# A streaming encoder step on one core: second-norm stage re-ordered, last taps and low parts on GpSimd, y rows ordered by expert block

## The chip, the core and the metric

The kernel is written for one core of one Trainium2 chip. A core has TensorE (matrix products into PSUM), VectorE, ScalarE, GpSimd and SyncE, which issues most DMAs. The engines run their own instruction streams and wait for each other on semaphores. In the views they are PE (PEld for its weight loads), DVE, ACT, POOL and SP; a queue name with a q behind it is that engine's sequencer or DMA queue. The metric is the device time of one launch in microseconds.

## What is computed

One layer with pre-norms, 1088 tokens (1024 of a prompt, 64 of a sample) of width 1024, all in fp32:

```
z = rms_norm(x, norm1_g) @ w_in                       # 512 pooling, 512 value, 512 gate columns
y_pool, _ = pool_mix(z[:, :512], ...)                 # window means, per-group linear, scale
v = a * sigmoid(gate); h = depthwise_conv(v, width 31) + b
y_conv = swish(layer_norm(h))
x = x + concat(y_pool, y_conv) @ w_out + b_out
hm = rms_norm(x, norm2_g)
# top 1 of 4 groups, then top 2 of its 8 experts; p_grp * normalised top_p are the gates
y = sum over the two chosen experts e of gate_e * ((silu(hm @ w_eg[e]) * (hm @ w_eu[e])) @ w_ed[e])
out = rms_norm(x + y, norm_f_g)
```

The last rows of the pooling input and of the convolution input are outputs too.

## The kernel before

Tokens are tiled by 128 rows: `NT` = 9 tiles, the last of 64. A product of two fp32 matrices is made of three: each operand is split into a high part (ScalarE copies it to the PE's format) and a low part (value less high part, by VectorE or GpSimd), and TensorE adds high x high, high x low and low x high. So every weight and every activation costs ScalarE a copy and another engine a subtraction.

Each engine's program is written out by hand; nothing is scheduled by a tool. The stages:

- **Input projection.** `turn_x(t)` transposes the nine normalised tiles; `in_proj(j, n)` multiplies column chunk j (12 of 128 columns, `KINDS`) with token block n (512, 512, 64). `in_proj(0, 0)` stands inside the loop of the transposes, all others after it. Chunks 0 and 1 use different PSUM banks.
- **Convolution.** Four groups of 128 channels, 31 taps. VectorE runs the taps of the parts `PART` by `taps`, one instruction a tap. For the ranges in `HELPED`, ScalarE makes the products of a tap (`products`) and GpSimd adds them (`additions`), with three product buffers `taps_pr` and the semaphores `prod_done` and `help_done`. Before, part C (group 1, its last 206 columns) is VectorE's.
- **Second-norm stage** (about 225 to 419 us). For each tile `out_conv(t)` and `out_pool(t)` make the output projection, 24 products each, from the parts in `part_h[t % 2]` and `part_l[t % 2]`. `residual(t)` (VectorE, L1256) adds x; ScalarE takes the sum of squares (L679) and the root (L682), written in the loop over t; `hm_row(t)` (L1263, L1268) scales the row; `turn_hm(t)` (TensorE, L943) transposes it; `hm_turned(t)` (ScalarE, L656) copies it out of PSUM; `logits(t)` (L954) are the router's products. `route(t)` and `count(t)` on VectorE find the two experts; `ranks(t)` (L964, L965) counts the rows ahead; `place(t)` (L1317 to L1335) turns ranks to slots; `slot_table` gathers all of it. `mix_high(t)` (ScalarE, L644, L650), `mix_conv_low(t)` and `mix_pool_low(t)` (VectorE, L1221, L1227) make the parts of tile t. The LayerNorm of token blocks 1 and 2 stands in the same stage: `ln_mean` (L817), `ln_center`, `ln_square`, `ln_variance` (L825), `ln_deviation`, `ln_normal`, `ln_swish`. `ln_mean(1)` waits for all taps. In the loop, TensorE makes `logits(t - 2)` and `ranks(t - 3)` after the output projection of tile t.
- **Experts.** 32 blocks of 128 rows, one for each expert; further blocks only if an expert has more than 128 rows (none here). `pair_loop` runs 15 passes of two blocks, then reads the number of pairs, then runs nine passes whose body is skipped, then a last pair is finished outside. TensorE works on one block after the other; its down projection is L1035 to L1037. GpSimd gathers rows for a block from `hm_scratch` (L1639) and scatters results (L1644) to `y2_dram`, where row 2 x token + k is the token's k-th expert.
- **Tail.** SyncE waits for `sc_all`, which GpSimd raises when the last scatter has landed, and loads both y rows of a tile with one DMA (`load_y2`, eight buffers). `combine(t)` (L1496) adds gate times row twice, ScalarE takes squares and root (L767, L770), `final(t)` (L1503, L1505) scales, SyncE stores.

## Time and profile before

| | us |
|---|---|
| median of 3 runs | 1084.33 (1083.77 to 1084.92) |
| the profiled execution | 1084.51 |
| its span, first to last instruction | 1082.8 |
| PE busy | 933.9 (86%) |
| DVE busy | 877.2 (81%) |
| ACT busy | 622.4 (57%) |
| POOL busy | 262.3 (24%) |
| mean granted TensorE clock | 0.927 of full speed |

A timeline row gives start and busy time of one instruction or of several alike (x count); what stands in brackets is the idle time of that engine ahead of it and the engine, tile and line whose work ended the wait. "issue" is time in which the profile shows nothing waited for. Groups by line give the total and the mean of one instruction. PEclk is the part of TensorE's full clock (2.4 GHz) that was granted; at half of it a product on 512 columns follows the last after 0.43 us, at full after 0.23.

### The profile page before, as it was taken

The page shows a single profiled execution, that of the slowest core. Times are in us where ns is not written, and L with a number is a line of the kernel's source. Part 1 is how long each engine was busy: PE and PEld are TensorE (multiplying, and loading weights), DVE is VectorE, ACT ScalarE, POOL GpSimd, SP SyncE. Part 2 cuts the span into 40 slices and gives each one's busy share as a digit, 9 for nine tenths or more (in the row PEclk, how much of TensorE's full clock was granted, in tenths as well). Part 3 has the DMA queues.
Part 4 walks back from the last instruction along what each step waited for, and adds up shares of the span by engine and source line. Part 5 has one row for each costly group of instructions (what it writes and reads, how often), then busy time and mean ns, then how long its engine had stood idle before and what let it go on. Part 6 is the DMA issues. An engine that isn't in the chain of part 4 may idle for free.

```text
span 1082.8 us, 13490 instructions
## 1 busy us (share of the span) xinstructions
PE 933.9 (86%) x4446; PEld 766.9 (71%) x4446; DVE 877.2 (81%) x974; ACT 622.4 (57%) x592; POOL 262.3 (24%) x284
## 2 busy tenths in 40 slices
PE   4999999791699983979999999999999999999710
PEld 3788888570468872768888888888888888888500
DVE  6279998979647875989898989898988989898248
ACT  7245353530232222747878787878787878887223
POOL 2158688350001101032212121212121111111000
PEclk8999999996889985889999999999999999999865
DMA  8211111131116242789999999999999999999466
GB/s 262 84 53 35 37 35 59 26 112 39 74 43 233 107 175 85 239 295 391 375 390 375 395 382 398 389 386 387 382 384 373 386 380 385 375 385 349 158 271 232
DMA packets 66299, 268.63 MB, mean 248 GB/s; under 512 B 15215, under 2 KB 28015, under 8 KB 40601
## 3 DMA queue, kind: packets, MB, share of 16 engines
q1 hardware_dynamic: 56761, 250.36, 61.9%
q0 software_dynamic: 9504, 17.85, 4.3%
q8 instruction: 18, 0.29, 0.1%
q14 instruction: 16, 0.13, 0.0%
HBM read 254.09 MB, written 30.86 MB: 263 GB/s over the span
## 4 chain that ended last, share of the span: by engine, by line
PE 81%; DVE 8%; issue 4%; ACT 3%; DMA 2%; SPq 0%; DVEq 0%; POOLq 0%; POOL 0%; ACTq 0%
PE ps L1021 11%; PE ps L1023 11%; PE ps L1022 11%; PE ps L899 8%; PE ps L1035 6%; PE ps L1036 6%; PE ps L1037 6%; PE ps L779 5%; PE ps L780 5%; PE ps L781 5%; PE ps L1010 3%; DVE arena L1496 2%; DVE ps L1155 2%; PE ps L1042 1%; PE ps L954 1%
## 5 line engine op out<-in xcount | busy, mean ns | idle before, releaser
L704 ACT ACTIVATE big<-arena 128x2048 fp32r<-128x2048 f32 x192 | 363.1, 1914 | 70.6 <-PE ps L1037 36.9
L1431 DVE TENSOR_TENSOR low<-arena,big 128x2048 fp32r<-128x2048 f32 x126 | 285.2, 2286 | 39.9 <-ACT big L704 37.2
L1021 PE MATMUL ps<-big,ring 128*128 128x512 f32 x512 | 205.5, 401 | 2.4 <-DVE ring L1436 2.4
L1023 PE MATMUL ps<-big,ring 128*128 128x512 f32 x512 | 201.2, 393 | 0.0
L1431 DVE TENSOR_TENSOR big<-arena,big 128x2048 fp32r<-128x2048 f32 x66 | 151.0, 2289 | 18.1 <-ACT big L704 14.7
L1155 DVE SCALAR_TENSOR_TENSOR ps<-arena,cols,ps 128x512 f32<-128x512 f32 (+1 forms) x174 | 137.2, 788 | 6.0
L1021 PEld LDWEIGHTS ps<-big,ring 128*128 128x128 f32 x512 | 97.0, 189 | 22.6 <-DVE ring L1436 2.8
L1023 PEld LDWEIGHTS ps<-big,ring 128*128 128x128 f32 x512 | 96.8, 189 | 22.5
L899 PE MATMUL ps<-big,ring 128*128 128x512 f32 (+1 forms) x432 | 104.7, 402 | 8.4 <-ACT arena L591 3.9
L1035 PE MATMUL ps<-big,hT 128*128 128x512 f32 x256 | 103.0, 402 | 8.9 <-DVE hT L1446 8.9
L779 PE MATMUL ps<-big,ring 128*128 128x512 f32 (+1 forms) x288 | 104.0, 361 | 0.4 <-DVE big L1119 0.4
L780 PE MATMUL ps<-big,ring 128*128 128x512 f32 (+1 forms) x288 | 102.7, 357 | 0.0
L781 PE MATMUL ps<-big,ring 128*128 128x512 f32 (+1 forms) x288 | 102.0, 355 | 0.0
L899 PEld LDWEIGHTS ps<-big,ring 128*128 128x128 f32 (+1 forms) x432 | 80.2, 188 | 30.7 <-ACT arena L591 4.7
L1037 PE MATMUL ps<-big,hT 128*128 128x512 f32 x256 | 101.9, 398 | 0.0
L1022 PE MATMUL ps<-low,ring 128*128 128x512 f32 x256 | 100.7, 394 | 0.0
L1022 PE MATMUL ps<-big,ring 128*128 128x512 f32 x256 | 100.6, 393 | 0.0
L1036 PE MATMUL ps<-low,hT 128*128 128x512 f32 x248 | 98.6, 397 | 0.0
L1661 POOL COPY cur<-s_idx 128x1 uint32 x32 | 16.7, 523 | 325.3 <-ACT arena L722 325.3
L1609 POOL TENSOR_TENSOR arena<-arena 128x606 f32<-128x606 f32 (+1 forms) x60 | 70.8, 1180 | 7.8 <-POOL arena L1609 0.4
L679 ACT ACTIVATE arena<-arena 128x1024 f32<-128x1024 f32 (+1 forms) x9 | 9.5, 1059 | 105.7 <-DVE arena L1256 84.0
L1035 PEld LDWEIGHTS ps<-big,hT 128*128 128x128 f32 x256 | 49.0, 191 | 20.9 <-DVE hT L1446 7.5
(228 smaller groups left out, 1409.2 us busy)
## 6 DMA issues: line engine op xcount, KB each, us to landing
arena<-in_w_eg SPq DMA_DIRECT2D x64, 1024.0 KB, 7.6
arena<-in_w_eu SPq DMA_DIRECT2D x64, 1024.0 KB, 7.0
arena<-in_w_ed SPq DMA_DIRECT2D x64, 1024.0 KB, 7.2
arena<-in_x_prompt SPq DMA_DIRECT2D x16, 512.0 KB, 5.4
y_in<-y_scratch SPq DMA_DIRECT2D x8, 1024.0 KB, 12.7
arena<-in_w_in SPq DMA_DIRECT2D x12, 512.0 KB, 3.6
arena<-in_w_out SPq DMA_DIRECT2D x8, 512.0 KB, 4.0
x_scratch<-arena SPq DMA_DIRECT2D x8, 512.0 KB, 2.6
```

What stands on the lines that cost most here:

```text
L704: act.activation(we_h[n % RING], raw[n % RING], ACT.Copy).then_inc(high_done, 1)
L779: pe.matmul(out, sh, mh, start=(i == 0), stop=False)
L780: pe.matmul(out, sh, ml, start=False, stop=False)
L899: ins = pe.matmul(out_ps[t % 2][0:r, c0:c0 + BANK], sh[t % 2][:, k, 0:r], mv[:, k, c0:c0 + BANK], start=(first and k == rows[0] and i == 0 ...
L1021: pe.matmul(out, part_h[b][:, k, :], wh[:, q, :], start=(k == 0), stop=False)
L1022: pe.matmul(out, part_h[b][:, k, :], wl[:, q, :], start=False, stop=False)
L1023: ins = pe.matmul(out, part_l[b][:, k, :], wh[:, q, :], start=False, stop=(k == KD - 1))
L1035: pe.matmul(out, hT_h[:, k, :], wh[:, q, c0:c0 + BANK], start=(k == 0), stop=False)
L1036: pe.matmul(out, hT_h[:, k, :], wl[:, q, c0:c0 + BANK], start=False, stop=False)
L1037: ins = pe.matmul(out, hT_l[:, k, :], wh[:, q, c0:c0 + BANK], start=False, stop=(k == KF - 1))
L1155: dve.scalar_tensor_tensor(to, v_ext[:, c, a + j:b + j], cols[:, c, j:j + 1], run, ALU.mult, ALU.add).then_inc(conv_step, 1)
L1431: dve.tensor_tensor(we_l[n % RING], raw[n % RING], we_h[n % RING].bitcast(F32), ALU.subtract).then_inc(low_done, 1)
```

## The change

1. `HELPED` has a third range, the former part C: its products are ScalarE's (31, in two pieces around the first row deviation) and its sums GpSimd's (13 and 17 additions, ahead of the additions of `b_out` to tiles 1 and 2). They use three product buffers of their own.
2. `in_proj(1, 0)` stands ahead of the transposes of the last tile.
3. The order of the second-norm stage is written out on TensorE, ScalarE and VectorE. The taps of group 3 are cut otherwise (8, 5, 18 instead of 10, 21), the low parts of tile 2 stand before the last 18. The LayerNorm means come after `out_pool(2)`. `logits(t - 1)` stands behind `out_pool(t)` from tile 5 on. The low parts of tiles 4 to 8 are made by GpSimd (`mix_low`).
4. In `place`, the two rows of a token are exchanged (`swap`, `rowv`) where the first expert's block has the higher number, so that k = 0 is always the lower block; seven instructions exchange the gates accordingly.
5. `pair_loop` enters the further passes only if there is one.
6. The tail loads the k = 0 rows of all tiles once all scatters but the last have landed, and the k = 1 rows after the last; `combine` is cut in two, nine additions for k = 0 first. 18 buffers instead of 8.

```diff
@@ -157,10 +159,13 @@
-FB = 8
...
-y_in = [place(f"y_in{s}", AT_BIG + s * HP, 2 * D)[:, :] for s in range(FB)]
+y_at = [[AT_BIG + (2 + t // 2) * HP + (t % 2) * D for t in range(NT - 1)] + [AT_ARENA + LOW_AT[1] * HP],
+        [AT_BIG + (0, 1, 6, 7)[t // 2] * HP + (t % 2) * D for t in range(NT - 1)] + [AT_ARENA + LOW_AT[1] * HP + D]]
+y_in = [[place(f"y_in{k}_{t}", y_at[k][t], D)[:, :] for t in range(NT)] for k in range(2)]
@@ -296,8 +303,8 @@
-PART = {"A": (0, BANK), "B": (BANK, HW_), "C": (CUT, HW_)}
-HELPED = [(0, BANK, HW_), (1, BANK, CUT)]
+PART = {"A": (0, BANK), "B": (BANK, HW_)}
+HELPED = [(0, BANK, HW_), (1, BANK, CUT), (1, CUT, HW_)]
@@ -336,10 +343,13 @@
-    with eng.Fori(PAIRS - 1, MAX_PAIRS - 1) as i:
-        with eng.If(rest > i):
-            body(i, True)
+    with eng.If(rest > PAIRS - 1):
+        with eng.Fori(PAIRS - 1, MAX_PAIRS - 1) as i:
+            with eng.If(rest > i):
+                body(i, True)
+            eng.nop()
...
+    eng.nop()
@@ -480,18 +490,18 @@
-    def load_y2(t):
-        r = ROWS[t]
-        sp.dma_start(y_in[t % FB][0:r, :], y2_dram[2 * t * P:2 * (t * P + r), :]
-                     .rearrange("(p k) n -> p (k n)", k=2)).then_inc(f_in[t % FB], 16)
...
+    def load_y2(k, t):
+        src = y2_dram[2 * t * P:2 * (t * P + ROWS[t]), :].rearrange("(p k) n -> p k n", k=2)[:, k, :]
+        sp.dma_start(y_in[k][t][0:ROWS[t], :], src).then_inc(f_in[k][t], 16)
...
+    sp.wait_ge(scat, 32 * rest + 32)
+    for t in range(NT):
+        load_y2(0, t)
...
-    for t in range(FB):
-        load_y2(t)
     for t in range(NT):
-        if t + FB < NT:
-            sp.wait_ge(f_acc, 2 * t + 2)
-            load_y2(t + FB)
+        load_y2(1, t)
+    for t in range(NT):
@@ -564,7 +574,7 @@
-                act.wait_ge(help_done, TAPS)
+                act.wait_ge(help_done, h * TAPS)
         for j in range(made[h], made[h] + n):
@@ -573,7 +583,7 @@
-                act.activation(taps_pr[j % 3][:, 0:b - a], v_ext[:, c, a + j:b + j], ACT.Copy,
+                act.activation(taps_pr[3 * (h == 2) + j % 3][:, 0:b - a], v_ext[:, c, a + j:b + j], ACT.Copy,
@@ -669,31 +679,43 @@
     for t in (0, 1):
...
-    for t in range(NT):
+    def row_deviation(t):
...
-        if t in (0, 2):
-            act.wait_ge(var_done, t + 1)
-        act.activation(junk[0:r, :], xt[t % 2][0:r, :], ACT.Square,
-                       accum_out=stat[0:r, 3, t:t + 1]).then_inc(sum2_done, 1)
+        if t == 4:
+            act.wait_ge(var_done, 3)
+        to = junk_h if t < 4 else junk
+        act.activation(to[0:r, :], xt[t % 2][0:r, :], ACT.Square, accum_out=stat[0:r, 3, t:t + 1]).then_inc(sum2_done, 1)
...
-        if t == 1:
-            mix_high(t + 2)
-            ln_square(1)
-            ln_square(2)
-        if t == 2:
-            ln_deviation(1)
-            ln_deviation(2)
-        if t >= 1:
-            hm_turned(t - 1)
-        if t == 2:
-            ln_swish(1)
-            ln_swish(2)
-        if t != 1 and t + 2 < NT:
...
+    products(2, 14)
+    row_deviation(0)
+    mix_high(2)
+    products(2, TAPS - 14)
+    row_deviation(1)
+    mix_high(3)
+    ln_square(1)
+    ln_square(2)
+    hm_turned(0)
+    row_deviation(2)
+    ln_deviation(1)
+    ln_deviation(2)
+    ln_swish(1)
+    ln_swish(2)
+    mix_high(4)
+    row_deviation(3)
+    hm_turned(1)
+    mix_high(5)
+    hm_turned(2)
+    for t in range(4, NT):
+        row_deviation(t)
+        hm_turned(t - 1)
+        if t + 2 < NT:
@@ -837,10 +859,14 @@
+        if t == NT - 2:
+            pe.wait_ge(wl_done, 2)
+            pe.wait_ge(cols_done, 1)
+            in_proj(1, 0)
     for n in (1, 2):
...
-    pe.wait_ge(cols_done, 1)
...
     def taken(j):
@@ -854,7 +880,7 @@
-        for n in range(3):
+        for n in range(1 if j == 1 else 0, 3):
@@ -978,29 +1004,56 @@
-    for t in range(NT + 3):
-        if 2 <= t < NT:
-            out_conv(t)
-            out_pool(t)
-        if t == 2:
-            pe.wait_ge(yp_dve, 3)
-            pe.wait_ge(conv_done, 3)
-            pe.wait_ge(help_done, 2 * TAPS)
-            ln_mean(1)
-            ln_mean(2)
-        if 3 <= t < NT + 2:
-            logits(t - 2)
-        if 1 <= t <= NT:
-            turn_hm(t - 1)
-        if t == 2:
-            pe.wait_ge(cen_done, 3)
-            ln_variance(1)
-            ln_variance(2)
-            logits(0)
-        if t == NT + 1:
-            slot_table("own", 0, 2 * NT - 6)
-        if t >= 3:
-            ranks(t - 3)
+    out_conv(2)
+    out_pool(2)
+    pe.wait_ge(yp_dve, 3)
+    pe.wait_ge(conv_done, 2)
+    pe.wait_ge(help_done, 3 * TAPS)
+    ln_mean(1)
+    ln_mean(2)
+    turn_hm(0)
+    out_conv(3)
+    pe.wait_ge(cen_done, 3)
+    ln_variance(1)
+    ln_variance(2)
+    out_pool(3)
+    logits(0)
+    turn_hm(1)
+    out_conv(4)
+    logits(1)
+    turn_hm(2)
+    out_pool(4)
+    logits(2)
+    turn_hm(3)
+    out_conv(5)
+    logits(3)
+    ranks(0)
+    turn_hm(4)
+    out_pool(5)
+    logits(4)
+    ranks(1)
...
+    out_pool(8)
+    logits(7)
+    ranks(6)
+    turn_hm(8)
+    logits(8)
+    slot_table("own", 0, 2 * NT - 6)
+    ranks(7)
+    ranks(8)
...
     def turn_rows(blk):
@@ -1247,7 +1300,7 @@
-    taps(10, ("B", 3))
+    taps(8, ("B", 3))
     def residual(t):
@@ -1329,44 +1382,77 @@
+        step(dve.tensor_tensor(swap[:, t:t + 1], s_b[:, a:a + 1], s_b[:, a + 1:b], ALU.is_gt))
+        dve.tensor_tensor(rowv[:, a:a + 1], tokv[:, a:a + 1], swap[:, t:t + 1], ALU.add)
+        step(dve.tensor_tensor(rowv[:, a + 1:b], tokv[:, a + 1:b], swap[:, t:t + 1], ALU.subtract))
...
         for s in (a, b - 1):
-            ins = dve.tensor_scalar(hots[s], iota[:, :], lane[:, s:s + 1], tokv[:, s:s + 1], ALU.is_equal,
+            ins = dve.tensor_scalar(hots[s], iota[:, :], lane[:, s:s + 1], rowv[:, s:s + 1], ALU.is_equal,
...
-    for t in range(NT + 3):
-        if t == 2:
-            ln_center(1)
-            ln_center(2)
-        if t < NT:
-            residual(t)
-            hm_row(t)
-        if t == 0:
-            pooled_sample()
-            taps(TAPS - 10, ("B", 3))
-            dve.wait_ge(conv_step, steps[0])
-            dve.engine_nop().then_inc(conv_done, 1)
-            taps(10, ("C", 1))
-        if t == 1:
-            taps(TAPS - 10, ("C", 1))
-            dve.wait_ge(conv_step, steps[0])
-            dve.engine_nop().then_inc(conv_done, 1)
-        if t == 2:
-            ln_normal(1)
-            ln_normal(2)
-        if t + 2 < NT:
-            mix_conv_low(t + 2)
-            mix_pool_low(t + 2)
-        if 2 <= t < NT + 2:
-            route(t - 2)
-            count(t - 2)
-        if t >= 3:
-            place(t - 3)
...
+    residual(0)
+    hm_row(0)
+    pooled_sample()
+    taps(5, ("B", 3))
+    mix_conv_low(2)
+    mix_pool_low(2)
+    taps(TAPS - 13, ("B", 3))
+    dve.wait_ge(conv_step, steps[0])
+    dve.engine_nop().then_inc(conv_done, 1)
+    residual(1)
+    hm_row(1)
+    mix_conv_low(3)
+    mix_pool_low(3)
+    ln_center(1)
+    ln_center(2)
+    residual(2)
+    hm_row(2)
+    ln_normal(1)
+    ln_normal(2)
+    residual(3)
+    route(0)
+    count(0)
+    hm_row(3)
+    route(1)
+    count(1)
+    residual(4)
+    hm_row(4)
+    route(2)
+    count(2)
+    route(3)
+    count(3)
...
+    residual(8)
+    place(5)
+    hm_row(8)
+    route(7)
+    count(7)
+    place(6)
+    route(8)
+    count(8)
+    place(7)
+    place(8)
     def slots(a, b):
@@ -1421,6 +1507,14 @@
+        step(dve.tensor_tensor(gtmp[:, 0, :], gates[:, 1, :], swap[:, :], ALU.mult))
+        step(dve.tensor_tensor(gtmp[:, 1, :], gates[:, 0, :], swap[:, :], ALU.mult))
+        step(dve.tensor_scalar(swap[:, :], swap[:, :], -1.0, 1.0, ALU.mult, ALU.add))
+        dve.tensor_tensor(gates[:, 0, :], gates[:, 0, :], swap[:, :], ALU.mult)
+        step(dve.tensor_tensor(gates[:, 1, :], gates[:, 1, :], swap[:, :], ALU.mult))
+        dve.tensor_tensor(gates[:, 0, :], gates[:, 0, :], gtmp[:, 0, :], ALU.add)
+        step(dve.tensor_tensor(gates[:, 1, :], gates[:, 1, :], gtmp[:, 1, :], ALU.add))
@@ -1488,14 +1582,15 @@
-    def combine(t):
-        r, s = ROWS[t], t % FB
-        dve.wait_ge(f_x[t], 16)
-        dve.wait_ge(f_in[s], 16 * (t // FB + 1))
-        for k in range(2):
-            dve.scalar_tensor_tensor(x_in[t][0:r, :], y_in[s][0:r, k * D:(k + 1) * D], gates[0:r, k, t:t + 1],
-                                     x_in[t][0:r, :], ALU.mult, ALU.add).then_inc(f_acc, 1)
-            dve.wait_ge(f_acc, 2 * t + k + 1)
+    def combine(k, t):
+        r = ROWS[t]
+        if k == 0:
+            dve.wait_ge(f_x[t], 16)
+        else:
+            dve.wait_ge(f_acc, t + 1)
+        dve.wait_ge(f_in[k][t], 16)
+        dve.scalar_tensor_tensor(x_in[t][0:r, :], y_in[k][t][0:r, :], gates[0:r, k, t:t + 1],
+                                 x_in[t][0:r, :], ALU.mult, ALU.add).then_inc(f_acc, 1)
     def final(t):
@@ -1621,10 +1718,26 @@
     for q in POOL_WO:
...
+    def mix_low(t):
+        r, tok = ROWS[t], t * P
+        pool.wait_ge(mixc_high, t + 1)
+        pool.tensor_tensor(part_l[t % 2][:, NG:KD, 0:r], hc[:, :, hc_at(tok):hc_at(tok) + r],
+                           part_h[t % 2][:, NG:KD, 0:r].bitcast(F32), ALU.subtract).then_inc(mixc_low, 1)
+        pool.wait_ge(mh_done, t + 1)
+        pool.tensor_tensor(part_l[t % 2][:, 0:NG, 0:r], u_ext[:, :, tok:tok + r],
+                           part_h[t % 2][:, 0:NG, 0:r].bitcast(F32), ALU.subtract).then_inc(ml_done, 1)
...
     for t in range(NT):
...
+        if t == 1:
+            additions(2, 13)
+        if t == 2:
+            additions(2, TAPS - 14)
+        if t >= 4:
+            mix_low(t)
```

Line numbers of the changed kernel differ: L925 is the output projection (L899 before), L980 the logits (L954), L969 the transposes of the norm row (L943), L990 and L991 the ranks (L964, L965), L691 and L693 square and root (L679, L682), L666 the copy `hm_turned` (L656), L654 and L660 the high parts, L495 the y loads.

TensorE's stream at tile 6, before: the output projection, the logits of tile 4, the transposes of tile 5, the ranks of tile 3.

```order
L899 MATMUL ps<-big,ring 128x512 [waits x2_done,mixc_low]
L899 MATMUL ps<-big,ring 128x512 x23
L899 MATMUL ps<-big,ring 128x512 [waits ml_done]
L899 MATMUL ps<-big,ring 128x512 x23
L954 MATMUL ps<-w_rt,arena 128x36 [waits lg_read,hmT_done]
L954 MATMUL ps<-w_rt,arena 128x36 x7
L943 MATMUL ps<-ident,arena 128x128 [waits hmT_done,hm_done]
L943 MATMUL ps<-ident,arena 128x128 x7
L964 MATMUL ps<-MS,tri 128x32 [waits placed,counted]
L965 MATMUL ps<-pref,ones 128x32
```

The same engine around tile 6 in the changed kernel, from `out_pool(5)` on: the logits that follow are those of the tile before (4, behind tile 5's products).

```order
L925 MATMUL ps<-big,ring 128x512 [waits ml_done]
L925 MATMUL ps<-big,ring 128x512 x23
L980 MATMUL ps<-w_rt,arena 128x36 [waits lg_read,hmT_done]
L980 MATMUL ps<-w_rt,arena 128x36 x7
L990 MATMUL ps<-MS,tri 128x32 [waits placed,counted]
L991 MATMUL ps<-pref,ones 128x32
L925 MATMUL ps<-big,ring 128x512 [waits x2_done,mixc_low]
L925 MATMUL ps<-big,ring 128x512 x23
L990 MATMUL ps<-MS,tri 128x32 [waits placed,counted]
L991 MATMUL ps<-pref,ones 128x32
L969 MATMUL ps<-ident,arena 128x128 [waits hmT_done,hm_done]
L969 MATMUL ps<-ident,arena 128x128 x7
```

Logits and ranks moved ahead by one tile, and the logits that follow a tile's products read a copy made later than before. That copy on ScalarE, changed kernel, tile 5: square and root of tile 5, then the copy of tile 4's transposed row, then the high parts of tile 7.

```order
L691 ACTIVATE arena,stat<-arena 128x1024 [waits sum2_done,x2_done]
L693 ACTIVATE stat<-stat,eps 128x1 [waits sum2_done]
L666 ACTIVATE arena<-ps 128x1024 [waits lg_done,hmtr_done]
L654 ACTIVATE ring<-arena 128x512 [waits out_done,mix_done]
L660 ACTIVATE ring<-arena 128x512
```

ScalarE's order inside a tile did not change there: the copy stands behind the square, which waits for the residual (`x2_done`).

SyncE's stream in the tail, before: both y rows of a tile in one load, all after the last scatter.

```order
L481 DMA bo_bc<-in_norm_f_g 128x1024
L485 DMA y_in_60<-y_scratch 128x2048 [waits scattered]
L485 DMA y_in_61<-y_scratch 128x2048
L485 DMA y_in_62<-y_scratch 128x2048
...
L485 DMA y_in_60<-y_scratch 64x2048 [waits f_acc]
L497 DMA out<-arena 128x1024 [waits f_y] x8
L497 DMA out<-x_last 64x1024 [waits f_y]
```

And in the changed kernel: nine loads wait for the scatter's count, nine for the last scatter.

```order
L491 DMA bo_bc<-in_norm_f_g 128x1024
L498 ISA
L495 DMA y_in_0_61<-y_scratch 128x1024 [waits scat]
L495 DMA y_in_1_62<-y_scratch 128x1024
...
L495 DMA y_in_8_69<-y_scratch 64x1024
L495 DMA y_in_0_70<-y_scratch 128x1024 [waits scattered]
L495 DMA y_in_1_71<-y_scratch 128x1024
...
L495 DMA y_in_8_78<-y_scratch 64x1024
L507 DMA out<-arena 128x1024 [waits f_y] x8
L507 DMA out<-x_last 64x1024 [waits f_y]
```

The first half of the loads moved ahead of the last scatter; each load is half as large.

## Rows read from the trace of the kernel before

**Rows 1.** Windows: length, busy PE, PEld, DVE, ACT, POOL (count), PEclk, DMA, GB/s.
```profile
36.00:206.00 170.00, 168.37 (x868) 140.83 (x866) 134.03 (x173) 67.78 (x100) 116.39 (x101) 0.99 0.12 36
232.00:297.00 65.00, 32.73 (x128) 24.32 (x126) 53.11 (x75) 8.83 (x14) 7.97 (x4) 0.79 0.13 51
...
325.00:419.00 94.00, 84.91 (x463) 71.60 (x461) 74.61 (x291) 28.57 (x41) 11.69 (x6) 0.90 0.40 149
484.00:1003.00 519.00, 519.00 (x2436) 428.97 (x2434) 464.70 (x261) 413.29 (x304) 89.88 (x118) 1.00 0.99 382
...
1031.00:1083.00 52.00, 0.46 (x2) 0.02 (x1) 35.50 (x36) 15.20 (x29) 1.16 (x2) 0.53 0.68 262
```

**Rows 2.** Timeline of PE at the head.
```profile
32.05 1.91 PE L792 MATMUL ps<-ident,arena 128*128 128x128 f32 x16
35.55 0.68 PE L792 MATMUL ps<-ident,arena 64*128 64x64 f32 x8 [1.59 <-DVE big L1119]
36.58 0.51 PE L779 MATMUL ps<-big,ring 128*128 128x512 f32 x1 [0.36 <-DVE big L1119]
...
38.19 0.63 PE L781 MATMUL ps<-big,ring 128*128 128x512 f32 x1
```

**Rows 3.** Timeline of PE around the second norm.
```profile
269.47 12.88 PE L899 MATMUL ps<-big,ring 128*128 128x512 f32 x48 [3.15 <-DVE ring L1221]
286.78 6.12 PE L817 MATMUL ps<-arena,mean_w 128*128 128x512 f32 x16 [4.44 <-issue]
...
325.94 11.25 PE L899 MATMUL ps<-big,ring 128*128 128x512 f32 x48
337.03 1.87 PE L954 MATMUL ps<-w_rt,arena 128*128 128x36 f32 x16
```

**Rows 4.** Groups by line and form, taps: count | busy us, mean ns | idle before.
```profile
L1609 POOL TENSOR_TENSOR arena<-arena 128x606 f32<-128x606 f32 x30 | 42.5, 1416 | 3.6
...
L1609 POOL TENSOR_TENSOR arena<-arena 128x400 f32<-128x400 f32 x30 | 28.3, 944 | 4.2 <-POOL arena L1609 0.4
...
L1155 DVE SCALAR_TENSOR_TENSOR arena<-arena,cols 128x206 f32<-128x206 f32 x30 | 15.0, 500 | 1.0
```

**Rows 5.** Timeline of DVE and ACT after the last tile's output projection.
```profile
393.41 1.22 DVE L1256 TENSOR_TENSOR arena<-ps,arena 64x1024 f32<-64x1024 f32 x1 [2.21 <-PE ps L899]
...
394.66 1.06 ACT L679 ACTIVATE arena<-arena 64x1024 f32<-64x1024 f32 x1 [10.36 <-DVE arena L1256]
...
396.04 1.00 ACT L656 ACTIVATE arena<-ps 128x1024 f32<-128x1024 f32 x1
```

**Rows 6.** Timeline of DVE, first read of the slot table.
```profile
418.69 0.19 DVE L1373 TENSOR_SCALAR idx_f<-ps 128x32 f32<-128x32 f32 x1 [0.70 <-PE ps L977]
```

**Rows 7.** Timeline of PE, first down projection.
```profile
470.69 0.80 PE L1035 MATMUL ps<-big,hT 128*128 128x512 f32 x1 [7.45 <-DVE hT L1446]
```

**Rows 8.** Timeline of all engines, loop exit to the first y tile.
```profile
1002.25 1.92 ACT L704 ACTIVATE big<-arena 128x2048 fp32r<-128x2048 f32 x1 [1.82 <-issue]
...
1017.71 0.98 POOL L1644 DMA_INDIRECT y_scratch<-arena,cur  x1 [0.83 <-POOL cur L1661]
...
1021.62 1.11 PE L1042 MATMUL ps<-ident,arena 128*128 128x128 f32 x4 [6.22 <-issue]
...
1034.08 0.97 POOL L1644 DMA_INDIRECT y_scratch<-arena,cur  x1 [0.81 <-POOL cur L1661]
...
1037.37 8.38 SPq L485 DMA_DIRECT2D y_in<-y_scratch  x9
...
1042.66 5.25 DVE L1496 SCALAR_TENSOR_TENSOR arena<-y_in,gates,arena 128x1024 f32<-128x1024 f32 x4 [18.57 <-DMA y_in<-y_scratch]
```

**Rows 9.** Timeline of DVE, a tile of the tail.
```profile
1049.56 2.60 DVE L1496 SCALAR_TENSOR_TENSOR arena<-y_in,gates,arena 128x1024 f32<-128x1024 f32 x2
...
1052.39 1.28 DVE L1505 SCALAR_TENSOR_TENSOR arena<-arena,stat,bo_bc 128x1024 f32<-128x1024 f32 x1
```

**Rows 10.** Timeline of DVE, a cast of a placing step.
```profile
349.94 2.29 DVE L1325 CAST sl<-sl_i 128x2 f32<-128x2 int32 x1
```

More of the change, by code:

```diff
@@ L1150, in taps @@
                         j = at_tap.get((part, c), 0)
[L1151 removed]
+                        run = acc_ps[:, 0:b - a]
                         if j:
@@ new lines, in _ @@
+            ln_normal(2)
[11 more added lines that the diff above has]
+            count(3)
+            residual(5)
+            place(0)
+            hm_row(5)
+            place(1)
+            route(4)
+            count(4)
+            residual(6)
+            place(2)
+            hm_row(6)
```

47 lines of the change are left out of this document (37 added, 10 removed).

## The prediction

> **What bounds the kernel now.** I read the busy times of stretches first [rows 1]. In 36 to 206 us (input projection) TensorE is busy 168.4 of 170 us: whatever starts it earlier moves everything behind it. In 484 to 1003 us (30 of 32 expert blocks) it is busy 519 of 519 us at a granted clock of 1.00, and no line of that loop's body changes. What is left is slack: 232 to 297 us holds 32.7 us of TensorE work in 65, with VectorE at 53.1; 325 to 419 us runs at 84.9 of 94; 1031 to 1083 us is a tail in which only VectorE (35.5) and ScalarE (15.2) work. So the change is priced in four places, as shifts of the chain. Times are those of the trace of before. The profiled execution took 1084.51 us (span 1082.8), the median is 1084.33: the sum is made against 1084.5, and the 0.2 between them is nothing here.
>
> **Head: one product moved ahead of the last transposes.** TensorE ends the transposes of tiles 6 and 7 at 33.96, idles 1.59, turns tile 8, idles 0.36, and its next eight or so products run at a start-to-start distance of 0.43 us, not 0.23 (durations 0.63 for 0.39) [rows 2]. With in_proj(1, 0) put there, 24 products (5.5 us) fill the wait for tile 8. Its inputs are ready (low part of chunk 1 at 27.7 us). Removed: 1.95 us of idle and 8 x 0.2 = 1.6 us of half clock, together 3.6. The bounds are 1.9 (clock falls anyway) and 3.8. The sigmoid, the weight parts and VectorE's gating of chunk 0 start 1.8 us later and still come before chunk 2 needs them (ready 54.2, needed 56.5). All of 36 to 206 us follows TensorE, so I take **-3.6**.
>
> **Second-norm stage, first half.** TensorE starts the LayerNorm means at 286.78 after 4.4 us of idle [rows 3], released by VectorE's taps of part C. These are 30 taps of 0.50 us and a first one [rows 4], 16.4 us with their spacing; they leave VectorE. The second tile's residual, its wait and its norm row (1.22 + 1.54 + 2.1, the first two as in [rows 5]) move behind the means: 4.9 more. Against it, ScalarE now makes 14 products before the first row deviation, in step with GpSimd: its 10th addition must be over. An addition on 206 elements I take from the two widths [rows 4]: busy 1.416 us at 606 and 0.944 at 400 is 2.3 ns an element, so 0.50, and 0.62 with the gap seen between them; GpSimd starts at 232.6, so ScalarE is free at 239.3, 0.8 late for x2. Means at 286.8 - 16.4 - 4.9 + 0.8 = 266.3. GpSimd's 30 additions end at 235 + 30 x 0.62 = 253.6, 12 us before they are asked for. Their cover is that; they cost nothing up to 1.03 us each.
>
> From 266.3 I go forward with durations of before: means 6.1, one transpose 1 to 2, out_conv(3) 5.7 (end 280), variance 3.9, out_pool(3) (289.4), logits 1.7. Beside it VectorE: residual(1), norm row(1), low parts(3), centring to 275.6, reciprocal and scaling 284.2 to 290.8. ScalarE: swish to 294.1, high part of tile 4. GpSimd now makes the low part of tile 4, 1.25 us (half of its 2.4 for 1024 elements), so out_conv(4) starts at 296.1 after 4 us of idle. Before it started at 325.94 [rows 3]: **-29.9** to this point.
>
> **Second half: routing one tile behind.** Before, the steady tile is 14.07 us: 48 products 11.1, logits 1.7, transposes 0.9, ranks 0.4 [rows 3], and logits(t-2) after out_pool(t) find their input long ready. Now logits(t-1) follow out_pool(t), while ScalarE's order is still row_deviation(t), hm_turned(t-1). So for t = 5, 6, 7, 8 TensorE waits for residual(t), square, root and copy, of which all but the copy belong to a tile it has only just finished. This chain is in the trace once, at tile 8: the residual starts at 393.41 as the products end, the square at 394.66, the copy runs 396.04 to 397.04 [rows 5]: 3.7 to 3.9 us. In 5, 6 and 7 (the fourth stands in the tail) it is 11.7 us. After idles of 2.5 to 4.4 us the next products run at half clock for a while: 48 of them took 12.88 after 3.15 us idle and 11.25 without [rows 3], +1.6. I charge that after each of three stalls and at out_conv(4): 6.4, with 0.6 for slower logits. From out_conv(4) to the end of out_pool(8) TensorE then has 5 x 11.1 products, 6 each of logits, transposes and ranks (18.4, where before had 4 sets, 12.1), 11.7 of stalls and 7.0 of clock: 92 against 67.3 before, **+24.6**.
>
> From there VectorE is the chain: residual, place(5), norm row, route(7), place(6), route(8), place(7), place(8). Before it takes 25.3 us to the table's reading at 418.69 [rows 6], with one route and one place more; each place now has three instructions more, two dependent steps, 0.5 us. The sum is 22.3: **-3.0**. The stage as a whole: -29.9 + 24.6 - 3.0 = **-8.3** (the gather and the first experts follow the table as before).
>
> The seven new instructions on the gates stand ahead of the low part that ends in the hidden low part for which TensorE waited 7.45 us [rows 7]. Five steps of 0.21 and two of 0.07 by their neighbours (0.17 busy): **+1.2**.
>
> **Loop exit and tail.** Between its last loop product (1015.4) and 1021.62 TensorE's sequencer runs nine skipped passes, 6.22 us; ScalarE passes the same nine in 1.82 [rows 8]. The fixed part (leaving, loading the count) is at most those 1.82; one guard replaces nine passes, so it gives 8/9 of 6.22 - 1.82 to 6.22: 3.9 to 5.5, I take 4.7. The Trainium skill (Advanced Engine Details and Errata, Control Flow Timing) gives 108 ns for a compare-and-branch and 51 ns for a branch, from which I estimate 1.4 us for nine passes and a gain of 1.3: the row shows four times that on TensorE, and by the page the time would be 3.4 us higher.
>
> Then: last scatter issued by 1035.05 before, now 1030.1; landed 2.3 us later, as before (1037.37), so 1032.4, and the second halves of y are asked for. The first halves wait only for the scatter of the block before, issued by 1018.7 [rows 8], landed 1021.0. Before, the first y tile took 5.3 us from issue to use (1042.66) and nine of 1 MB were issued in 8.4 us [rows 8]; a half tile I put at 4.5, then 1.38 us a tile by the loop's 382 GB/s [rows 1]. VectorE, free since 1019, adds the nine first halves in 1.3 us each, to 1037.9. Second halves arrive from 1037 on. I start their chain at 1039 (between 1037.9 and 1041, since the last scatter shares the queues with the first halves). Then nine times 1.3 + 1.41 (addition, reciprocal and scaling; before 2.60 + 1.43 = 4.03 a tile [rows 9]), 1.5 for the root's table, 0.2 at the end: 26.1. End at 1065.1 against 1079.36: **-14.2**, loop exit included.
>
> **Sum:** -3.6 - 8.3 + 1.2 - 14.2 = -24.9, so 1084.5 - 24.9 = **1059.5**.
>
> **Rivals.** (a) The clock stays up across the stalls, or they cost less: for it, in [rows 2] three products ran at full clock after the idle before it fell, so the fall may hit the short logits and not the products; against it, the 48 products behind 3.15 us of idle were slow [rows 3]. 7 us less: 1052.5. (b) The split of y gives nothing: the last scatter stands behind 4.5 MB of first halves, or these land as late as before. Only the loop exit is left of the tail, -4.7: 1069. Against it: 14 us lie between 1021 and 1035. (c) VectorE and GpSimd get in each other's way. A cast of 0.17 us took 2.29 while GpSimd added b_out to a row of 1024 [rows 10]; GpSimd's work goes from 2.4 to 4.9 us a tile, and 30 additions lie beside VectorE's norm rows. One such blocking of some 2.3 us in the chain of two or three tiles: +5, 1064.5. The Trainium skill (SBUF — State Buffer, two separate sides) states it as a rule: VectorE and GpSimd share a port pair, held for a whole instruction, also against a VectorE operation with two SBUF inputs; the row agrees for the cast. (d) Slower than before: ScalarE and GpSimd hand over product and sum one by one, and the means wait for the last sum at 235 + 30x. From x = 1.03 us it costs, from (266.3 + 27.1 - 235) / 30 = 1.95 us the kernel is slower by over 0.2%: 1087. Against it stands 1.08 us for twice the width. (e) The change moves nothing: the wait for the last taps is taken over by something I don't see, and the stalls eat the rest: 1084.
>
> **Chances.** Forecast 0.54, (a) 0.13, (b) 0.14, (c) 0.13, (d) 0.04, (e) 0.02. The likeliest is 1059.5. Range 1049 to 1069: the upper end takes in (b) and (c), the lower one (a) with the best of the head (3.8) and exit (5.5) and a tail chain from 1037.9. A measurement of this kernel tells about 0.2% from no change: faster by more than that 0.94, within it 0.02, slower 0.04.
>
> **What would show it.** Head: no gap between tile 7's transposes and the products, chunk 1 done near 56.5. Stage: means near 263 on the new clock of events (266.3 less the head's 3.6), out_conv(4) near 292.5, and idle of 3.7 to 3.9 us before the logits of tiles 4 to 7, with the following products at half clock. Exit: TensorE's 6.2 us gap near 1.5. Tail: first-half loads landing before the last scatter, VectorE's period 2.7 us. I am wrong if additions on GpSimd take over 1 us, if the logits don't stall (then the time is under 1050), or if the second halves land after 1041 less the shifts.

## The result, and the profile of the changed kernel

The changed kernel takes 1069.93 us (1069.39 to 1073.12, 4 runs) against 1084.2: ratio 0.9874, 95% interval 0.9858 to 0.989. That is 13.7 us less by the ratio, where the forecast had 24.9 less and a range up to 1069, 0.9 below the measured time. Sign right, size missed: eleven microseconds of the expected gain did not come. The profiled execution took 1070.19 us (span 1068.4).

The stretches that answer to [rows 1] (length, then busy time of PE, PEld, DVE, ACT and POOL with counts, granted clock, DMA share, GB/s), in the trace of the changed kernel:

```profile
33.00:203.00 170.00, 168.57 (x886) 141.26 (x884) 136.14 (x174) 70.02 (x102) 116.55 (x102) 1.00 0.13 40
232.00:294.00 62.00, 48.73 (x203) 36.19 (x201) 49.10 (x64) 29.46 (x56) 24.45 (x31) 0.86 0.23 85
...
327.00:417.00 90.00, 68.60 (x308) 56.04 (x308) 56.39 (x253) 20.47 (x28) 13.77 (x8) 0.75 0.24 85
470.00:1000.00 530.00, 530.00 (x2476) 438.17 (x2475) 475.38 (x268) 419.12 (x308) 90.23 (x118) 1.00 1.00 382
1028.00:1068.00 40.00, 0.00 (x0) 0.00 (x0) 31.96 (x34) 14.18 (x28) 0.11 (x1) 0.50 0.77 286
```

Much of the slack before 294 us is gone, as meant: TensorE does without work for 13 us of 62, where it was 32 of 65. But 327 to 417 us, where before it was busy 84.9 of 94 us at a mean granted clock of 0.90, now has it busy 68.6 of 90 at 0.75: the second half of the stage has become the slow part. TensorE's timeline there (start, length, engine, line, form, count, idle before and its releaser):

```profile
34.09 0.48 PE L801 MATMUL ps<-big,ring 128*128 128x512 f32 x1
...
264.76 7.32 PE L839 MATMUL ps<-arena,mean_w 128*128 128x512 f32 x16 [3.11 <-issue]
...
294.47 7.27 PE L925 MATMUL ps<-big,ring 128*128 128x512 f32 x24 [3.55 <-POOL ring L1725]
...
320.80 5.75 PE L925 MATMUL ps<-big,ring 128*128 128x512 f32 x24
330.35 2.28 PE L980 MATMUL ps<-w_rt,arena 128*128 128x36 f32 x16 [3.79 <-ACT arena L666]
...
333.28 8.25 PE L925 MATMUL ps<-big,ring 128*128 128x512 f32 x24
...
352.11 3.45 PE L980 MATMUL ps<-w_rt,arena 128*128 128x36 f32 x16 [3.79 <-ACT arena L666]
...
356.22 7.11 PE L925 MATMUL ps<-big,ring 128*128 128x512 f32 x24
...
373.45 3.63 PE L980 MATMUL ps<-w_rt,arena 128*128 128x36 f32 x16 [3.73 <-ACT arena L666]
...
377.74 8.14 PE L925 MATMUL ps<-big,ring 128*64 128x512 f32 x24
...
396.42 3.39 PE L980 MATMUL ps<-w_rt,arena 128*128 128x36 f32 x16 [3.78 <-ACT arena L666]
...
415.92 0.61 PE L1003 MATMUL ps<-hot_mem 128*128 128x32 f32 x2 [2.53 <-DVE hot_mem L1392]
```

L925 is the output projection, L980 the logits. Four idles of 3.73 to 3.79 us stand before the logits of tiles 4 to 7, released by ScalarE's copy (L666). Behind each, 16 logit products take 2.28 to 3.63 us (1.87 elsewhere) and 24 projection products 7.11 to 8.25 (5.75 elsewhere). ScalarE's timeline at the first of them shows why the copy is late: it stands behind square (L691) and root (L693) of the tile just finished.

```profile
327.91 1.06 ACT L691 ACTIVATE arena<-arena 128x1024 f32<-128x1024 f32 x1 [13.26 <-DVE arena L1309]
...
329.09 0.29 ACT L693 ACTIVATE stat<-stat,eps 128x1 f32<-128x1 f32 x1
329.29 1.00 ACT L666 ACTIVATE arena<-ps 128x1024 f32<-128x1024 f32 x1
```

Loop exit and tail in the timelines of PE, POOL and DVE (first down projection; exit; last scatter; first halves of y, which L1592 adds; the first second halves; the steady tile):

```profile
469.40 0.79 PE L1088 MATMUL ps<-big,hT 128*128 128x512 f32 x1 [8.62 <-DVE hT L1540]
...
1014.87 0.65 PE L1095 MATMUL ps<-ident,arena 128*128 128x128 f32 x4 [0.39 <-issue]
...
1026.80 1.31 POOL L1757 DMA_INDIRECT y_scratch<-arena,cur  x1 [0.80 <-POOL cur L1774]
...
1034.92 2.67 DVE L1592 SCALAR_TENSOR_TENSOR arena<-y_in,gates,arena 128x1024 f32<-128x1024 f32 x2 [1.59 <-DMA y_in<-y_scratch]
...
1039.71 2.63 DVE L1592 SCALAR_TENSOR_TENSOR arena<-y_in,gates,arena 128x1024 f32<-128x1024 f32 x2 [0.39 <-DMA y_in<-y_scratch]
...
1045.22 1.28 DVE L1592 SCALAR_TENSOR_TENSOR arena<-y_in,gates,arena 128x1024 f32<-128x1024 f32 x1
...
1047.81 1.28 DVE L1592 SCALAR_TENSOR_TENSOR arena<-y_in,gates,arena 128x1024 f32<-128x1024 f32 x1
```

The exit gap of 6.22 us [rows 8] is 0.39, and the steady tile of the tail takes 2.59 us instead of 4.03 [rows 9].

### The profile page after: what moved, and what is told of

Read it like the earlier page. It is cut to its first block, busy times and chain, and to the rows that moved or that the text cites. A ratio compares the mean times of both kernels' runs of the same rounds, so it can differ in the third digit from the quotient of the medians.

```text
span 1068.4 us, 13431 instructions
## 1 busy us (share of the span) xinstructions
PE 945.7 (89%) x4446; PEld 774.7 (73%) x4446; DVE 865.0 (81%) x967; ACT 635.7 (59%) x623; POOL 293.1 (27%) x324
## 4 chain that ended last, share of the span: by engine, by line
PE 84%; DVE 6%; ACT 3%; DMA 3%; issue 3%; POOL 1%; SPq 0%; DVEq 0%; POOLq 0%; ACTq 0%
PE ps L1076 11%; PE ps L1074 11%; PE ps L1075 11%; PE ps L925 8%; PE ps L1088 6%; PE ps L1090 6%; PE ps L1089 6%; PE ps L801 5%; PE ps L802 5%; PE ps L803 5%; PE ps L1063 3%; PE ps L980 2%; PE ps L1095 1%; PE ps L839 1%; DMA arena<-hm_scratch,g_idx 1%
## 5 line engine op out<-in xcount | busy, mean ns | idle before, releaser
L925 PE MATMUL ps<-big,ring 128*128 128x512 f32 (+1 forms) x432 | 113.4, 423 | 14.0 <-DVE ring L1274 7.1
L925 PEld LDWEIGHTS ps<-big,ring 128*128 128x128 f32 (+1 forms) x432 | 84.6, 199 | 38.6 <-DVE ring L1274 7.5
L801 PE MATMUL ps<-big,ring 128*128 128x512 f32 (+1 forms) x288 | 103.6, 360 | 0.0
L802 PE MATMUL ps<-big,ring 128*128 128x512 f32 (+1 forms) x288 | 102.2, 355 | 0.0
L803 PE MATMUL ps<-big,ring 128*128 128x512 f32 (+1 forms) x288 | 101.6, 354 | 0.0
L1774 POOL COPY cur<-s_idx 128x1 uint32 x32 | 12.2, 382 | 323.7 <-ACT arena L744 323.7
L1706 POOL TENSOR_TENSOR arena<-arena 128x606 f32<-128x606 f32 (+2 forms) x90 | 89.4, 993 | 12.0 <-POOL arena L1706 0.4
L586 ACT ACTIVATE arena<-arena,cols 128x606 f32<-128x606 f32 (+2 forms) x90 | 54.7, 630 | 39.1 <-POOL arena L1706 39.1
```

The lines of the kernel that those rows point to most:

```text
L801: pe.matmul(out, sh, mh, start=(i == 0), stop=False)
L802: pe.matmul(out, sh, ml, start=False, stop=False)
L803: ins = pe.matmul(out, sl_, mh, start=False, stop=(i == len(parts) - 1 and last))
L925: ins = pe.matmul(out_ps[t % 2][0:r, c0:c0 + BANK], sh[t % 2][:, k, 0:r], mv[:, k, c0:c0 + BANK], start=(first and k == rows[0] and i == 0 ...
```

## The experiments

All ratios are against the kernel before, on the same chip; microseconds behind them are the ratio times 1084.33. The changed kernel is 1070.7 on that scale (0.9874). **The theory** after the result: the ends of the program (head, exit, tail) carry the whole gain, and the re-ordered stage gives back nearly all it wins, because ScalarE's order makes TensorE wait once a tile, and each wait costs nearly as much again in clock. **Its rivals**: the stage worked and other parts fell short; the waits are VectorE's or GpSimd's and would come anyway; the slow clock lies beside other waits and costs nothing.

**The stage taken out, and alone.** e1_rest is the changed kernel with the stage as before; e4_stage is the kernel before with the new stage only (the diff's pieces on tap products, part C, low parts and the orders of the four engines).

> The changed kernel with its second-norm stage as before the change (order of TensorE, ScalarE and VectorE, part C of the taps, low parts): head, loop guard, y by halves and the seven gate instructions remain. Theory (read from the two traces): these parts are worth 3.3 + 5.8 + 7.6 - 1.2 = 15.5 us, so 1068.7, and the reordered stage gives nothing, or costs about 1. Rival (the forecast's sum for the stage is right and other parts fell short): the stage gives 8.3 us, so without it 1078.

> The kernel before with the second-norm stage of the changed one, and no other part. Theory: +1 us or so (head start of 28 us to out_conv(4), 31 us given back, 1.4 gained at the end): 1085. Rival (the forecast's -8.3): 1076.

Measured: e1_rest 0.9881 (0.9854 to 0.9909), 1071.4 us; e4_stage 0.9986 (0.9974 to 0.9999), 1082.8 us. Without the stage the ratio is 0.0007 above the changed kernel's, 0.8 us, far within the intervals. Alone it is worth 1.5 us (0.1 to 2.8), not the 8.3 of the forecast, nor the small loss that I expected. So some 7 of the 11 us that failed to come are the stage's. The other parts together gave 12.9 (9.9 to 15.8), where the forecast's sum for them is 16.6 (3.6 and 14.2, less 1.2) and the traces have 15.5 (expectation of e1_rest); of that difference the traces show 1.1 us, told below, and the rest stays open.

**ScalarE's order swapped.** One tile's copy ahead of the next tile's square and root:

```
             for t in range(4, NT):
+                if t > 4:
+                    hm_turned(t - 1)
                 row_deviation(t)
-                hm_turned(t - 1)
+                if t == 4:
+                    hm_turned(t - 1)
                 if t + 2 < NT:
```

> The changed kernel, ScalarE copies the turned norm row of the tile before ahead of square and root of the tile just finished (tiles 5 to 8). Theory: this order alone causes the idles of 3.8 us before logits 4 to 7 and the slow clock behind them (periods of 21.7, 21.4 and 22.9 us). They fall to 14 to 15 us, about 22 us less, and logits 7 come 3 earlier: 1045 (1043 to 1049). Rival: TensorE waits for VectorE's rows anyway (VectorE has some 14 us of work a tile and GpSimd shares its port), periods of 18 or more: 1058 or above.

Measured: 0.9649 (0.9622 to 0.9676), 1046.3 us: 24 us below the changed kernel, from the order of two calls. TensorE's timeline in it, where the first idle was, and the longest idle left at the end:

```profile
327.47 1.87 PE L983 MATMUL ps<-w_rt,arena 128*128 128x36 f32 x16
...
329.71 5.76 PE L928 MATMUL ps<-big,ring 128*128 128x512 f32 x24
...
378.17 1.11 PE L972 MATMUL ps<-ident,arena 64*128 64x64 f32 x8 [4.08 <-DVE arena L1324]
...
393.56 0.61 PE L1006 MATMUL ps<-hot_mem 128*128 128x32 f32 x2 [2.52 <-DVE hot_mem L1395]
```

From the start of out_conv(4), 294.47 in both, the last product of the slot table comes at 393.56 for 415.92: 22.4 us. VectorE was not the limit for these tiles (it keeps TensorE waiting once, for 0.69 us, before the 4.08 above); the rival (1058 or above) falls.

**The waits kept, the clock kept up.** In e3_busy TensorE makes 16 products of no use in each of the four idles; nothing else moves:

```
+            def keep_busy(t):
+                pe.wait_ge(x2_done, t)
+                for _ in range(16):
+                    pe.matmul(out_ps[(t + 1) % 2][:, 0:BANK], wo_h[:, 0, 0:P], wo_h[:, 0, 0:BANK], start=True, stop=True)
...
             out_pool(5)
+            keep_busy(5)
             logits(4)
```

> The changed kernel with 16 products of no use (3.7 us at full clock) on TensorE in each of the four idles before logits 4 to 7; the order of all else is kept, so the waits of 3.8 us stay and only the clock behind them may differ. Theory: the clock is what the forecast undersized; logits at 1.9 us and 24 products at 5.8 after them give back 10 to 11.5 us: 1059. Rival: the slow products lie beside other waits (VectorE), and keeping the clock gives under 3 us: 1067 or more.

Measured: 0.9776 (0.9753 to 0.9799), 1060.0 us. The timeline of PE in it, at the first idle:

```profile
325.04 3.79 PE L964 MATMUL ps<-big 128*128 128x512 f32 x16
329.00 1.98 PE L985 MATMUL ps<-w_rt,arena 128*128 128x36 f32 x16 [0.17 <-ACT arena L666]
...
331.25 5.74 PE L925 MATMUL ps<-big,ring 128*128 128x512 f32 x24
```

The logits still start 4 us after the projection's end, but at full clock, and so do the 24 products behind them. Useless work of 15 us on TensorE made the kernel 10.6 us faster than the changed one (8 to 14 by the intervals). Of the 24 us that e2_swap gives, then, 10.6 are clock and some 14 the waits themselves; the rival (1067 or more) falls.

**Idles elsewhere filled.** On top of the swapped order, such products before out_conv(2), the means, out_conv(4), around the first gathered rows and before the first down projection:

> The kernel of the swapped ScalarE order (e2_swap: 1046.3 profiled), with products of no use wherever TensorE still idles over 2 us between out_conv(2) and the first experts' down projection: 26, 16 and 14 before out_conv(2), the means and out_conv(4), 22 and 9 around the first gathered rows, 34 before the first down projection. Theory: the slow products behind those idles are on the chain. Behind out_conv(4) 8.35 for 5.76 us and means and variance 1.7 earlier, together 4.3; behind the gathered rows 10 x 0.2 and behind the hidden rows 11 x 0.2, 4.2 more, less where VectorE is late anyway: 1040 (1038 to 1042.5). Rival: these stretches are bound by VectorE and the gather, and the clock there costs nothing: 1045 to 1047.

Measured: 0.9624 (0.9593 to 0.9655), 1043.6 us; the intervals of this and e2_swap overlap. The trace says where it helps and where not (PE timeline):

```profile
294.38 5.78 PE L928 MATMUL ps<-big,ring 128*128 128x512 f32 x24 [0.40 <-POOL ring L1742]
...
343.36 7.34 PE L928 MATMUL ps<-big,ring 128*128 128x512 f32 x24
...
393.33 0.61 PE L1011 MATMUL ps<-hot_mem 128*128 128x32 f32 x2 [2.52 <-DVE hot_mem L1409]
...
442.92 0.50 PE L1101 MATMUL ps<-big,hT 128*128 128x512 f32 x1 [0.78 <-DVE hT L1557]
```

Out_conv(4) took 5.78 us for the 8.35 of e2_swap, yet the table came at 393.33, only 0.2 earlier: of the 2.6 us, 0.7 went into a wait for VectorE's placing (before 342.92) and 1.6 into the 7.34 us at 343.36 (below). In the experts it holds: the first down projection starts 2.4 us earlier than in e2_swap (445.32), and the loop's exit comes 4.7 us earlier (985.90 for 990.59).

**The gate instructions moved out of the way.** The block of twelve that computes the gates goes into a function called ahead of the first addition of y.

> The kernel of the swapped ScalarE order, with all twelve instructions on the gates moved behind the expert loop, where VectorE waits 7.8 us for the first y tile. Theory (that of the forecast's +1.2): they stand in the chain to the first down projection, whose wait of 8.62 falls by 2.4 us, and the end comes 2.4 earlier: 1044. Rival: the loop behind is bound by the weights' transfer and takes the gain back: 1046.5, with the wait shorter all the same.

Measured: 0.9625 (0.9602 to 0.9649), 1043.7 us. The PE timeline has the wait at 6.24 for 8.62, as expected:

```profile
440.21 0.80 PE L1091 MATMUL ps<-big,hT 128*128 128x512 f32 x1 [6.24 <-DVE hT L1545]
```

The interval does not exclude a zero by itself, but from the first expert product to here this trace has 34.6 us and e2_swap 37.0, and the loop behind is no longer for it (544.8 us from here to its exit, 545.3 in e2_swap): the 2.4 stay. The instructions were on the path.

**Taps and low parts back on VectorE**, each on top of the swapped order. e7_capdve makes the 31 taps of part C with VectorE, ahead of residual(1); e8_lowdve gives it the low parts of tiles 4 to 8:

> The kernel of the swapped ScalarE order, with the 31 taps of part C back on VectorE (as before the change, 0.50 us each), ahead of the second tile's residual. Theory: the means wait for them, 15.6 us later than at 265.8, and all behind follows: 1062 (1060 to 1064). Rival: VectorE, no longer held by GpSimd's additions, and ScalarE without the 31 products make up part of it: 1057 or less.

> The kernel of the swapped ScalarE order, with the low parts of tiles 4 to 8 back on VectorE (1.3 us a tile). Theory: with TensorE busy 69 of 70 us from 300 to 370 us VectorE has room for them, GpSimd's two take 2.8 each for VectorE's 0.7, so out_conv(4) comes 2 to 4 us earlier and the rest is even: 1044 (1042 to 1046). Rival: VectorE is the next limit, five tiles of 1.3 us come on top: 1050 or more.

Measured: e7_capdve 0.9794 (0.9778 to 0.9811), 1062.0 us: 15.7 above e2_swap, about what the 31 taps take; the rival (1057 or less) falls. Against e6_gates on the same chip, with the same stage otherwise, its means start 14.7 us later (279.31 for 264.64). So moving part C to GpSimd is worth those 16 us once nothing behind it gives them back. e8_lowdve 0.9675 (0.9648 to 0.9703), 1049.1 us (1046.2 to 1052.1): my 1044 lies outside, the rival's 1050 is not excluded, and neither is no difference from e2_swap. Rows of e7_capdve (first) and e8_lowdve (second), PE and DVE timelines:

```profile
279.31 6.74 PE L840 MATMUL ps<-arena,mean_w 128*128 128x512 f32 x16 [20.31 <-issue]
```

```profile
295.70 7.62 PE L928 MATMUL ps<-big,ring 128*128 128x512 f32 x24 [4.87 <-DVE ring L1277]
...
296.47 2.07 DVE L1324 SCALAR_TENSOR_TENSOR arena<-arena,stat,g_bc 128x1024 f32<-128x1024 f32 x1
```

In the changed kernel the norm row beside GpSimd's low parts takes longer; its DVE timeline:

```profile
296.62 3.16 DVE L1321 SCALAR_TENSOR_TENSOR arena<-arena,stat,g_bc 128x1024 f32<-128x1024 f32 x1
```

So 3.16 us for 2.07: the two engines do get in each other's way, by 1.1 us here. But out_conv(4) came no sooner for it. It stands 28.6 us behind the start of the means (267.07), as in e2_swap (265.84 and 294.47), although the means ran faster here (4.51 us for 6.21); in e6_gates, where they also took 4.51, it is 27.4. With VectorE's low part of tile 4 ahead of it, out_conv(4) is 1.3 us later, not 2 to 4 earlier.

**The small parts one by one**, each on the kernel before:

> The kernel before with the guard around the overflow loop alone. Theory (the rows): TensorE's gap of 6.22 us at the loop exit falls to 0.4 to 0.9 and all behind follows, 5.5 us: ratio 0.995, 1078.8. Rival (an estimate from the Trainium skill, Advanced Engine Details and Errata, Control Flow Timing): 1.3 us, ratio 0.9988.

> The kernel before with y by halves, rows ordered by block, and the seven gate instructions; no guard, head or stage. Theory: first halves added before the last scatter has landed, 7.6 us less in the tail, gates 1.2 more: ratio 0.994, 1077.9. Rival (the forecast's b): the halves come no earlier than they are used: +1.2, ratio 1.001.

> The kernel before with the one product moved ahead of the last transposes. Theory: 3.3 us earlier at 206 us, and all behind follows: ratio 0.997, 1081.0. Rival: VectorE's taps, which end the wait before the means, do not start earlier, and the gain is gone by 290 us: ratio 1.000.

Measured: guard 0.994 (0.9925 to 0.9956), 6.5 us; tail with its gates 0.9933 (0.9918 to 0.9948), 7.3; head 0.9979 (0.997 to 0.9988), 2.3. The estimate of 1.3 us for the exit (ratio 0.9988) is outside; TensorE's gap there fell from 6.22 us to 0.57. The sum of the three is 16.1, together in e1_rest they gave 12.9: a difference that the intervals do not settle, but the traces show where guard and tail can overlap. Timelines of ACT and DVE in e11_tail, the last with ACT's row of the changed kernel behind it:

```profile
1048.96 2.53 DVE L1515 SCALAR_TENSOR_TENSOR arena<-y_in,gates,arena 128x1024 f32<-128x1024 f32 x2 [4.55 <-DMA y_in<-y_scratch]
...
1050.28 1.06 ACT L772 ACTIVATE arena<-arena 128x1024 f32<-128x1024 f32 x1 [11.65 <-DVE arena L1515]
```

```profile
1041.03 1.06 ACT L789 ACTIVATE arena<-arena 128x1024 f32<-128x1024 f32 x1 [15.48 <-DVE arena L1592]
```

Without the guard VectorE has added all first halves and waits 4.55 us for the second ones, which the last scatter (1040.37) holds up: its first square comes 9.9 us after that scatter. With the guard the scatter is early (1026.80), the second halves wait for the first ones (0.39 us of idle), and the square comes 14.2 after it. Whatever ends earlier in the tail, the nine first halves are the next limit.

**All that helped, together**: swapped order, filled idles (25 products in place of 34 before the first down projection), gates behind the loop.

> Everything that helped together: the swapped ScalarE order, the gate instructions behind the loop, and the products of no use (25 instead of 34 before the first down projection, since its wait is now 6.2 us). Theory: the gains of the two additions (2.6 and 2.7 by their ratios) are on one chain and add up, but the wait for the hidden rows is shared, so 4 to 5 on top of the swapped order's 0.9649: 0.9605, 1041. Rival: the loop behind is at its transfer limit and takes none of the second one: 0.9625.

Measured: 0.9571 (0.9558 to 0.9584), 1037.8 us, a larger gain than expected (1041): 46.5 us below the kernel before, 33 below the changed one, 8.5 below e2_swap. The down projection now begins 32.6 us behind the first expert product (37.0 in e2_swap), about half of that; the loop's exit comes 7.3 us earlier than in e2_swap (983.25 for 990.59). Its PE timeline and granted clock (windows) from the table to the loop:

```profile
407.71 0.50 PE L1087 MATMUL ps<-big,ring 128*128 128x512 f32 x1 [0.29 <-DVE ring L1549]
...
440.35 0.51 PE L1101 MATMUL ps<-big,hT 128*128 128x512 f32 x1 [0.42 <-DVE hT L1559]
```

```profile
392.00:445.00 53.00, 48.09 (x220) 39.38 (x221) 42.80 (x61) 25.74 (x19) 5.70 (x5) 0.91 0.69 237
```

## Why the prediction was off, by its own steps

**Head, -3.6: held in the trace.** The product starts at 34.09 at full clock, the stretch of 170 us ends 3.3 us earlier (202.89 for 206.16). Alone the part is worth 2.3 (1.3 to 3.3), which is inside the stated bounds of 1.9 to 3.8 but short of the 3.6.

**First half of the stage, -29.9: nearly held.** Means forecast at 262.7 in the changed kernel's own times, measured 264.76; out_conv(4) 292.5 and 294.47, so 28.2 us of the 29.9 came, and 0.3 less of the head. The 2.0 missing are there at the means already. These waited for VectorE's last tap of chunk 3, in the DVE timeline of the changed kernel:

```profile
263.76 0.84 DVE L1208 SCALAR_TENSOR_TENSOR arena<-arena,cols,ps 128x606 f32<-128x606 f32 x1
```

GpSimd's additions, in two runs of its timeline, had ended 10 us before, at 0.69 and 0.80 us each where I had 0.62. But they were not free. Beside them and the addition of `b_out` between the two runs, VectorE's first norm row took 2.83 us for the 1.98 of before, and a low part 1.04 for 0.68; in e7_capdve, with GpSimd idle at that time, that norm row takes 2.08. So 1.2 of the 2.0 us are GpSimd in VectorE's way, which the sum had at nothing and only rival (c) named. POOL and DVE timelines of the changed kernel, then DVE in e7_capdve:

```profile
239.77 2.83 DVE L1321 SCALAR_TENSOR_TENSOR arena<-arena,stat,g_bc 128x1024 f32<-128x1024 f32 x1
...
241.01 13.68 POOL L1706 TENSOR_TENSOR arena<-arena 128x206 f32<-128x206 f32 x17 [0.18 <-ACT arena L586]
```

```profile
238.79 2.08 DVE L1322 SCALAR_TENSOR_TENSOR arena<-arena,stat,g_bc 128x1024 f32<-128x1024 f32 x1
```

From the means to out_conv(4) it was 29.7 us for the 29.8 of the sum, and that was in part luck: e3_busy, the same program up to there, has its means at 264.73, runs them in 4.51 us for 7.32, and starts out_conv(4) at 292.09.

**Second half, +24.6: the step that failed.** Its three stalls were right to 0.1 us: 3.79 + 3.79 + 3.73 = 11.3 for 11.7. The term for the clock was not. I charged 1.6 us behind each of three stalls and at out_conv(4), 7.0 with the logits, from one row where 48 products took 1.6 longer after 3.15 us of idle [rows 3]. Measured, as time over that at full clock: logits 0.4 + 1.6 + 1.8, projections 2.5 + 1.3 + 2.4 and 1.5 at out_conv(4), ranks 1.2, 12.7 in all. The 1.6 us behind my price are some 8 products at low clock (0.2 each); here it was low from the logits on, through the ranks, and for up to a dozen of the next 24 products besides. From out_conv(4) to the end of out_pool(8) it is 98.2 us for the 92 forecast: +6.2. A slip of addition is in that too: the terms as written, 55.5 + 18.4 + 11.7 + 7.0, make 92.6. e3_busy confirms the term: with the clock kept in the stalls that stretch takes 88.3, though its out_conv(4) is 1.0 slower.

**End of the stage, -3.0: half.** 23.9 us to the table for 22.3, chiefly since logits 7 stand behind the fourth stall, at low clock (3.39 us), and VectorE waits for them before route(7):

```profile
399.84 0.16 DVE L1338 TENSOR_TENSOR lgt<-ps,b_rt 128x4 f32<-128x4 f32 x1 [0.92 <-PE ps L980]
```

I had put that stall "in the tail", as if covered. e2_swap, without it, needs 22.3 us (371.85 to 394.17), the forecast's number. Counted from the last residual, route(7) starts 7.1 us later with the stall and 6.0 without; most of the other half microsecond is one cast that took 1.01 us for 0.17 while GpSimd filled a row of 1024 (401.87 to 402.83), GpSimd in VectorE's way once more.

**Stage as a whole**: -8.3 forecast; by the traces +1.2 behind the head's part, alone on the chip 1.5 us faster (0.1 to 2.8).

**Gates, +1.2: held** (wait 8.62 for 7.45). **Loop exit, -4.7: 5.8 came** (0.39 for 6.22), as "one guard replaces nine passes" had it; I took the fixed part for larger than it is. The Trainium skill's prices (Advanced Engine Details and Errata, Control Flow Timing) led to an estimate of 1.3; the measurement is over four times that and decides. **Rest of the tail**: the second halves' chain began at 1039.71, which is 25.2 us after the loop's last product where the sum had 23.6. The nine first halves took 14.7 us from the first addition to the last (1024.67 to 1039.33) where the sum had 12.4: they arrived with gaps, the longest of 1.59 us at 1034.92. Exit and tail together -13.4 for -14.2; that this is so close is luck, since 1.1 more from the exit hides 1.9 less from the tail.

Added up: 9.8 late at the table (2.0 + 6.2 + 1.6) and 0.8 in exit and tail: 1059.5 + 10.6 = 1070.1, the profiled 1070.19. (Two more slips in the sum are small: 1084.5 - 24.9 is 1059.6, and the last scatter, 1035.05 less 4.7, is 1030.35 and not 1030.1, which is not on the chain.) The clock term's 5.7 us (12.7 for 7.0) are the largest single piece.

**The rivals.** (a), clock stays up, is what e3_busy built, and only with work put there. (b) did not happen; the tail gave its gain. (c) was real but small: 1.2 us ahead of the means and 0.8 at the cast near the end, some 2 of the 10.6. At the low parts of tiles 4 to 8 it cost nothing that e8_lowdve could win back, in spite of its row (3.16 us for 2.07). (d) is excluded by 0.69 to 0.80 us an addition. (e), to which I gave 0.02 for the whole kernel, is close to the truth for the stage alone: "the stalls eat the rest" is what happened, but only there. The range ended at 1069 because its upper end was made of (b) and (c); a bound for the clock term, which I left at a single value, was missing. In hindsight: had I let each of the four idles cost as much again as it lasts, 3.8 + 3.8 + 3.8 + 3.6 = 15.0 for the 7.0 charged, the forecast with that bound alone would have been 8 higher, 1067.5, and with (c) beside it 1072.5.

## What to carry to other kernels

When two engines hand a value back and forth once a tile, write down what each has queued ahead of the hand-over: two calls in the wrong order on the third engine cost 24 us here, more than the 13.7 that the changed kernel gained. Price an idle of TensorE of 3 to 4 us twice, once for itself and once for the clock behind it, and give the second part a range (here four idles of 14.9 us together had 12.7 us of slow clock behind them). And if such an idle can't be removed, products of no use in it may pay, provided that TensorE is what everybody waits for afterwards.
